# A third TensorE job body of 144 columns in a mixture-of-experts decoder layer

## What is computed

```python
top_v, top_e = lax.top_k(logits, TOP_K)              # 1024 rows x 4 experts of 32
hid = jnp.dot(xblk, w1[e]) + b1[e]                   # (rows of the expert, 1024) x (1024, 2048)
glu = jnp.minimum(hid[:, 0::2], SWIGLU_LIMIT)
lin = jnp.clip(hid[:, 1::2], -SWIGLU_LIMIT, SWIGLU_LIMIT)
act = glu * jax.nn.sigmoid(SWIGLU_ALPHA * glu) * (lin + 1.0)
return jnp.dot(act, w2[e]) + b2[e]                   # (rows, 1024) x (1024, 1024)
```

## Time and profile before

| | |
|---|---|
| median of 3 runs | 2070.32 us (2068.22 to 2071.92) |
| the profiled execution, time | 2069.33 us |
| the profiled execution, span | 2067.7 us |
| TensorE busy, share of the span | 95% |
| VectorE, ScalarE, GpSimd busy | 76%, 65%, 32% |
| mean granted TensorE clock | 0.982 |

### The profile page before, as it was taken

One profiled execution on the slowest core, in us unless ns is written; L12 is line 12 of the kernel. 1 busy time (PEld: TensorE's weight loads), 2 busy tenths in 40 slices (PEclk: granted clock), 3 DMA queues, 4 the chain that ended last, 5 costly groups with the idle time before them and its releaser, 6 DMA issues.

```text
span 2067.7 us, 39657 instructions
## 1 busy us (share of the span) xinstructions
PE 1965.6 (95%) x11170; PEld 1683.2 (81%) x11171; DVE 1580.4 (76%) x2202; ACT 1342.1 (65%) x1931; POOL 667.3 (32%) x758
## 2 busy tenths in 40 slices
PE   7999998879987999999999999999999999999995
PEld 6888877877765888889788897979897888979884
DVE  5334256875678788989888898889898888988886
ACT  5231156663437586877768777787778687777865
POOL 3100001321244142524325244344244252443423
PEclk9999999999978999999999999999999999999998
DMA  5323121113357898989899898999898998989987
GB/s 194 72 82 102 56 78 42 42 49 111 123 170 284 283 315 290 351 274 356 288 314 326 280 370 275 333 314 370 275 359 292 309 334 281 364 268 337 317 286 249
DMA packets 267760, 507.35 MB, mean 245 GB/s; under 512 B 39148, under 2 KB 44268, under 8 KB 267320
## 3 DMA queue, kind: packets, MB, share of 16 engines
q1 hardware_dynamic: 244042, 453.98, 63.8%
q0 software_dynamic: 23664, 52.67, 9.6%
HBM read 463.09 MB, written 43.53 MB: 245 GB/s over the span
## 4 chain that ended last, share of the span: by engine, by line
PE 64%; issue 1%; DMA 1%; ACT 1%; POOL 1%; DVE 1%; POOLq 0%; ACTq 0%; DVEq 0%
PE ps L1225 17%; PE ps L732 11%; PE ps L734 11%; PE ps L733 10%; PE ps L1227 7%; PE ps L1265 3%; PE ps L1266 3%; PE ps L1117 2%; PE ps L1198 1%; ACT whi L1591 0%; DMA raw<-acc_d,icur 0%; PE ps L1189 0%; DVE wlo L2277 0%; DMA acc_d<-y,icur 0%; ACT y L1622 0%
## 5 line engine op out<-in xcount | busy, mean ns | idle before, releaser
L2277 DVE TENSOR_TENSOR wlo<-raw,whi 128x1024 fp32r<-128x1024 f32 x764 | 912.8, 1219 | 110.1 <-ACT whi L1591 106.0
L1591 ACT ACTIVATE whi<-raw 128x1024 fp32r<-128x1024 f32 x764 | 830.4, 1117 | 134.3 <-PE ps L1227 93.0
L1225 PE MATMUL ps<-xT,whi 128*128 128x320 f32 x1920 | 504.6, 349 | 6.3 <-DVE wlo L2277 5.8
L1227 PE MATMUL ps<-xT,wlo 128*128 128x160 f32 x1920 | 456.0, 238 | 0.0
L1225 PEld LDWEIGHTS ps<-xT,whi 128*128 128x128 f32 x1920 | 363.2, 189 | 10.0 <-DVE wlo L2277 6.2
L1227 PEld LDWEIGHTS ps<-xT,wlo 128*128 128x128 f32 x1920 | 369.1, 192 | 0.5
L2627 POOL DMA_INDIRECT acc_d<-y,icur x93 | 161.2, 1733 | 443.7 <-ACT y L1625 258.5
L732 PE MATMUL ps<-whi,xT 128*128 128x512 f32 x544 | 218.1, 401 | 3.2 <-DVE wlo L2133 3.2
L732 PE MATMUL ps<-whi,aT 128*128 128x512 f32 x512 | 212.9, 416 | 3.0 <-DVE aTl L2333 3.0
L734 PE MATMUL ps<-whi,xT 128*128 128x512 f32 x544 | 213.2, 392 | 0.0
L733 PE MATMUL ps<-wlo,xT 128*128 128x512 f32 x544 | 212.8, 391 | 0.0
(11 more groups left out here) (348 smaller groups left out, 3553.5 us busy)
## 6 DMA issues: line engine op xcount, KB each, us to landing
raw<-in_w SPq DMA_DIRECT2D x768, 512.0 KB, 9.9
raw<-in_w_in SPq DMA_DIRECT2D x16, 512.0 KB, 5.9
xs<-in_x SPq DMA_DIRECT2D x8, 512.0 KB, 10.5
raw<-in_w_out SPq DMA_DIRECT2D x8, 512.0 KB, 3.8
mix<-in_x SPq DMA_DIRECT2D x8, 512.0 KB, 3.7
h_d<-h SPq DMA_DIRECT2D x8, 512.0 KB, 2.7
acc_d<-mix SPq DMA_DIRECT2D x8, 512.0 KB, 4.4
raw<-acc_d SPq DMA_DIRECT2D x8, 512.0 KB, 8.4
```

Source lines behind the costliest of these rows:

```text
L1225: pe.matmul(o2, wh[:, a, cols], xT2[:, :, k, 0:JOB_T], start=q == 0 and a == 0, stop=False, skip_group_check=True)
L1227: m = pe.matmul(o, wl[:, a, cols], xT2[:, 0, k, 0:JOB_T], start=False, stop=q == QUARTERS - 1 and a == 1, skip_group_check=True)
L1591: act.activation(parted(slot(whis, s)), paired(raw_slot(s), s), ACT.Copy).then_inc(split_hi, 1)
L2277: dve.tensor_tensor(parted(slot(wlos, s)), paired(raw_slot(s), s), parted(slot(whis, s).bitcast(F32)), ALU.subtract).then_inc(split_lo, 1)
```

## The change

A constant `NARROW = 144` is added, and TensorE's `job` takes a width. Jobs of 129 to 144 rows run a third written-out body, `job(j, 2, 144)`, in which the pair of `wide_step` moves 2 x 144 and 144 columns; jobs of 145 to 160 rows keep the body of 160. One more `If` chooses between them. The positions in PSUM stay those of 160 columns, so the second half of `o2` still begins at column 160, and columns 144 to 159 of each half hold what an earlier job left. ScalarE, VectorE, GpSimd and SyncE are not changed; the `w2` half is the same in both wide bodies.

```diff
+NARROW = 144
@@ TensorE
-            def job(j, blocks):
+            def job(j, blocks, width=JOB_T):
@@ wide_step
-                        o = ps[:, bank, 0:JOB_T]
-                        o2 = ps[:, bank, 0:2 * JOB_T].rearrange("p (h n) -> p h n", h=2)
+                        o = ps[:, bank, 0:width]
+                        o2 = ps[:, bank, 0:2 * JOB_T].rearrange("p (h n) -> p h n", h=2)[:, :, 0:width]
                         for a in range(2):
                             k = 2 * q + a
-                            pe.matmul(o2, wh[:, a, cols], xT2[:, :, k, 0:JOB_T], start=q == 0 and a == 0, stop=False,
+                            pe.matmul(o2, wh[:, a, cols], xT2[:, :, k, 0:width], start=q == 0 and a == 0, stop=False,
                                       skip_group_check=True)
-                            m = pe.matmul(o, wl[:, a, cols], xT2[:, 0, k, 0:JOB_T], start=False,
+                            m = pe.matmul(o, wl[:, a, cols], xT2[:, 0, k, 0:width], start=False,
                                           stop=q == QUARTERS - 1 and a == 1, skip_group_check=True)
@@ the loop over jobs
                             with pe.If(left < P + 1):
                                 job(j, 1)
                             with pe.Else():
-                                job(j, 2)
+                                with pe.If(left < NARROW + 1):
+                                    job(j, 2, NARROW)
+                                with pe.Else():
+                                    job(j, 2)
```

## The result

The changed kernel takes 2187.38 us (median of 4 runs, 2183.5 to 2191.75) where the kernel before takes 2071.12 us beside it: a ratio of 1.0565, 95% interval 1.0553 to 1.0578. The profiled execution has a span of 2190.1 us, 122.4 more than before.

What follows compares the result with a forecast made beforehand. TensorE's own pace was taken to bound the job loop; 22.2 us from shortened pairs plus 0.1 at low clock, other terms 0, took 2069.33 to 2047.0, plus 1.0 for the median: 2048. Range 2040 to 2302, likeliest case 2040 to 2060.

Steps and rivals of the forecast that it cites:

- The pair: TensorE's two matmuls of `wide_step`, start to start: 133 + 14 + 112 = 259 ns, against 260 measured.
- parts 1 and 2: The pair in wide jobs: first matmul at 2 x 144 columns saves 13.3 ns a pair, second at 144 nothing.
- the floor of 112 ns: On TensorE a matmul with a weight load of 128 columns ahead takes no less than 112 ns.
- Part 3: Which jobs shorten: 13 of 15 wide jobs, 1664 pairs, 22.2 us; each takes 51.3 us instead of 53.0.
- the sum: Total gain of 22.3 us, 22.2 from the warm pairs, against the profiled execution's 2069.33, giving 2047.0.
- Part 4: Whether VectorE's sums on 160 columns cover the gain in wide jobs: taken as 0, bound 0.4 us a job, 5 us.
- Part 5: The added `If` on TensorE's sequencer: about 0.2 us a wide job, hidden, so 0; uncovered 3 us.
- Part 6: TensorE's longer instruction list, 1716 for 1024: loop taken as kept, cost 0; first visit bound 8.2 us.
- rival 1: Loop no longer kept, code fetched anew at TensorE's branches at body ends, 8.2 us each: 2187 or more; chance 0.40.
- 17 narrow jobs, 2187: Case of rival 1: one 8.2 us branch in each of 17 narrow jobs, 139 us less 22, giving 2187.
- Rivals 2, 3 and 4: Weight loads set both matmuls, 2070, 0.04; both matmuls shrink, 2037, 0.03; VectorE's sums make wide jobs wait, 2053, 0.03.
- The signs: Wrong if pairs take 240 or 260 ns, long branches idle job starts with over 32 fetches, or idle ends with `gsum`.

Runs made afterwards that it cites:

- the run with the unused body: The changed kernel with the added `If`'s condition set never to hold, so the 144 body stands in the loop but is never run: 2087.05 us, ratio 1.0081.

## Why the prediction was wrong

It forecast 2048 us, and the kernel went to 2187. By its steps:

- **The pair, and parts 1 and 2.** Right in mechanism. The second matmul at 144 gave nothing, as the floor of 112 ns said; both at 144 gave 14.4 ns a pair where 13.3 was forecast. From the second unit on the pairs came in two paces, 243.3 and 246.7 ns: the second is the one forecast (246 to 247, from 260), the first is why the size was a little over.
- **Part 3.** Right: 13 jobs, busy for 51.0 to 51.6 us each but the first (53.2), for a forecast of 51.3. 24 us were there to be had for the 22.2 of the sum.
- **Part 4.** Right: VectorE's waits for TensorE went to almost nothing and no sum was late.
- **Part 5.** Right: with the loop kept, the branches of the added `If` are hidden. In the run with the unused body the later wide jobs take 53.0 us, as before.
- **Part 6.** This step failed. It set the forecast on the loop being kept, and the loop wasn't. The row that misled was true: no branch missed between the first job and the last. But it told of a round of seven blocks in a store of eight, and said nothing of a round of nine. The prediction asked whether 1716 instructions and the sequencer's fit, a question of length; the run with the unused body has the same length and is kept. Its rival 1 did say that the loop may touch one block too many, but no count followed. It had to count the blocks that a round enters, those ahead too, and the place of the loop in them. Counted so, with the place unknown, the changed loop makes a round of nine in 98 of 256 places, 0.38. The chance of 0.40 for this rival was about right, and a forecast that depends on a place it can't see should have said so.
- **Rival 1.** This is what happened, but its case "17 narrow jobs, 2187" hit the time by offsetting errors. It priced one branch of 8.2 us in 17 narrow jobs, 139 us. What ran were two branches in each of 13 wide jobs, 8.9 us of idle time and 2.2 us of low clock behind it, 144 us by the rows. The place was off: the narrow body's jump found the loop's end in store, because the wide job before had just brought it; the wide body's jump did not.
- **Rivals 2, 3 and 4.** None occurred. The pair has neither 240 nor 260 ns over a job, and no idle time ends with `gsum`.
- **The signs.** Idle time ahead of a job's first matmul, branches of several us and far more than 32 fetches were named as signs of the wrong case. "By about three" was too few: a round of nine fetches nine.

## What to carry to other kernels

Before a written-out body is added to a loop, count how many blocks of 256 instructions one round of that loop enters, with the block behind each piece, and where the loop begins in its block; on this chip eight were kept and nine cost 11 us a round. Share the part of a body that doesn't differ (here the `w2` half), and if a round still lands on nine, move the loop by some instructions that stand under an idle time. A profile in which a tuned engine has idle time put down to "issue", or to an engine that was done long before, is read on at its branches and its instruction fetches.

## What was not expected of the hardware

- A hundred instructions that only wait for what is already met moved the time by 130 us, and with 240 the loss was back.
- A branch into a block that wasn't there took 4.2 to 7.8 us while the weights streamed.
- A wait that is met is recorded with 51 ns, but in a row of a hundred their starts lay 108 ns apart.
- Pairs at 144 columns settle for a whole job into one of two paces, 243.3 or 246.7 ns from the second unit on, with no stop in between; at 160 there was one, 260.0. What chooses stays open.
